# Two softmax heads handled as a pair: transposes, copy, reciprocal and buffers of the attention stage of a two-layer trunk

## What is computed

```python
def one_block(args):                       # MLA, dense and causal
    qb, t0 = args
    q_pos = t0 + jnp.arange(Q_BLOCK)
    logits = jnp.einsum('bqhd,bshd->bhqs', qb, k).astype(jnp.float32) * scale
    visible = key_pos[None, :] <= q_pos[:, None]
    logits = jnp.where(visible[None, None], logits, NEG_INF)
    p = jax.nn.softmax(logits, axis=-1).astype(v.dtype)
    return jnp.einsum('bhqs,bshd->bqhd', p, v)
```

## Time and profile before

| | us |
|---|---|
| median of three runs | 1304.08 (1303.95 to 1306.27) |
| profiled execution, its own time | 1305.61 |
| its span, first to last instruction | 1303.9 |
| TensorE busy | 1255.1 (96% of the span) |
| VectorE busy | 773.8 (59%) |
| ScalarE busy | 540.4 (41%) |
| mean granted TensorE clock | 0.995 of full |

### The profile page before, as it was taken

The page is one execution under the profiler, slowest core; times in us unless marked ns, Lnnn a source line. Parts: engine busy times, 40 slices in busy tenths (PEclk is TensorE's granted clock), DMA queues, the critical chain, the costliest instruction groups (busy, mean ns, idle before and its releaser), DMA issues.

```text
span 1303.9 us, 19103 instructions
## 1 busy us (share of the span) xinstructions
PE 1255.1 (96%) x5916; PEld 983.1 (75%) x5916; DVE 773.8 (59%) x1240; ACT 540.4 (41%) x871; POOL 247.1 (19%) x157
## 2 busy tenths in 40 slices
PE   4999999899999999999999999988999999999997
PEld 3856777578888888888877568765888888888886
DVE  4579866734454454444766888575445445445458
ACT  4474435834413314224436643376442242231343
POOL 4022340011020020110531324200201201102016
PEclk9999999999999999999999999999999999999999
DMA  5312220023222222222232112200233223222223
GB/s 200 101 49 65 65 98 1 2 65 110 97 96 97 97 97 97 97 97 97 97 99 81 56 59 82 65 2 2 97 125 97 97 96 97 96 96 98 96 98 129
DMA packets 31023, 110.46 MB, mean 85 GB/s; under 512 B 3568, under 2 KB 3568, under 8 KB 30960
## 3 DMA queue, kind: packets, MB, share of 16 engines
q1 hardware_dynamic: 29088, 103.82, 24.0%
q0 software_dynamic: 576, 3.76, 0.8%
q10 hardware_dynamic: 1296, 2.12, 0.5%
HBM read 107.59 MB, written 2.10 MB: 84 GB/s over the span
## 4 chain that ended last, share of the span: by engine, by line
PE 89%; DVE 3%; ACT 3%; issue 3%; POOL 1%; DMA 1%; DVEq 0%; ACTq 0%; SPq 0%; POOLq 0%
PE bank L824 18%; PE bank L823 18%; PE bank L822 18%; PE bank L477 6%; PE bank L479 6%; PE bank L478 6%; PE bank L511 2%; PE bank L500 2%; PE bank L498 2%; PE bank L499 2%; PE bank L709 1%; PE bank L736 1%; PE bank L721 1%; PE bank L693 1%; POOL lnb L410 1%
## 5 line engine op out<-in xcount | busy, mean ns | idle before, releaser
L877 ACT ACTIVATE wh<-raw 128x1024 fp32r<-128x1024 f32 x194 | 204.8, 1056 | 397.3 <-PE bank L824 239.0
L1165 DVE TENSOR_TENSOR wl<-raw,wh 128x1024 fp32r<-128x1024 f32 x158 | 247.2, 1565 | 102.6 <-ACT wh L877 95.1
L822 PE MATMUL bank<-hh,wl 128*128 128x512 f32 x512 | 200.0, 391 | 0.0
L822 PE MATMUL bank<-xmh,wl 128*128 128x512 f32 x512 | 199.3, 389 | 0.0
L824 PE MATMUL bank<-hl,wh 128*128 128x512 f32 x512 | 199.2, 389 | 0.0
L824 PE MATMUL bank<-xml,wh 128*128 128x512 f32 x512 | 199.2, 389 | 0.0
L823 PE MATMUL bank<-xmh,wh 128*128 128x512 f32 x512 | 199.2, 389 | 0.0
L823 PE MATMUL bank<-hh,wh 128*128 128x512 f32 x512 | 199.2, 389 | 0.0
L445 POOL TENSOR_TENSOR x<-x,rsb 128x512 f32<-128x512 f32 x64 | 84.6, 1322 | 580.3 <-DVE rsb L1555 580.3
L477 PE MATMUL bank<-xgh,wl 128*128 128x512 f32 x368 | 152.7, 415 | 23.5 <-DVE xgl L1174 18.3
L1544 DVE TENSOR_TENSOR sqb<-tf 128x512 f32<-128x512 f32 x64 | 44.3, 693 | 181.3 <-ACT hh L1136 181.3
(11 more groups left out here) (190 smaller groups left out, 1747.6 us busy)
## 6 DMA issues: line engine op xcount, KB each, us to landing
raw<-in_stream SPq DMA_DIRECT2D x194, 512.0 KB, 3.3
x<-in_x ACTq DMA_DIRECT2D x8, 256.0 KB, 12.5
out_y<-x SPq DMA_DIRECT2D x8, 256.0 KB, 4.3
par<-in_params POOLq DMA_DIRECT2D x2, 916.0 KB, 4.9
con<-in_consts POOLq DMA_DIRECT2D x1, 944.5 KB, 9.2
par<-in_params POOLq DMA_DIRECT2D x1, 896.0 KB, 11.4
par<-in_params ACTq DMA_DIRECT2D x1, 20.0 KB, 1.8
```

Source lines behind the costliest of these rows:

```text
L822: pe.matmul(B.t[s][:], wl[:, s, n_block(k)], src_h[:, k], start=(k == 0), stop=False)
L877: act.activation(wh[:, s], raw[:, s], ACT.Copy).then_inc(hi_ready.sem, 1)
L1165: vec.tensor_tensor(wl[:, s], raw[:, s], wh[:, s], ALU.subtract).then_inc(lo_ready.sem, 1)
```

## The change

Slots are handled two at a time. T becomes `turn_pair`: both heads' blocks go into banks 4 and 5, which are one tensor `banks45`, and there is one use (`pt0` to `pt15`) instead of one for each slot. C becomes one copy of both banks. N becomes one reciprocal of 128x2 and the two products, behind a wait for both sums. Planes of probabilities go from four to six, of transposes they stay four. On TensorE the sums of squares go ahead of `gla_out` and W. The first output unit waits for the last copy by name.

```diff
-LEAD, LAG, PLANES = 3, 2, 4
+LEAD, LAG, PLANES = 3, 2, 6
-    + [(f"pt{j}", 4 + j % 2) for j in range(N_ATT)]
+    + [(f"pt{p}", 5) for p in range(N_ATT // 2)]
-        self.t = [ctx.enter_context(nc.psum_tensor(f"bank{b}", [P, T], F32)) for b in range(8)]
+        self.t = [ctx.enter_context(nc.psum_tensor(f"bank{b}", [P, T], F32)) for b in range(4)]
+        self.both = ctx.enter_context(nc.psum_tensor("banks45", [P, 2, T], F32))
...
-        place("mpad", [P, 2, T])
+        pb3, _ = place("pb3", [P, 2, T])
-        pt2, _ = place("pt2", [P, T], at=xh0 + 4 * MIXED[-1] * T)
-        pt3, _ = place("pt3", [P, T], at=xl0 + 4 * MIXED[-1] * T)
+        pt2, _ = place("pt2", [P, 2, KB * T], at=xh0 + 4 * MIXED[-1] * T)
...
-                def turn(j):
-                    name = f"pt{j}"
+                def turn_pair(j):
+                    name = f"pt{j // 2}"
                     pe.wait_ge(*B.vacant(l, name))
-                    pe.wait_ge(*pn_ready.at(l, j))
-                    for kb in range(part_of(j)[1] + 1):
-                        m = pe.transpose(B[name][:, kb * P:(kb + 1) * P],
-                                         probs(j)[:, kb * P:(kb + 1) * P], ident)
+                    if j == 0:
+                        pe.wait_ge(*B.freed(l, "inc00"))
+                    for hp in range(2):
+                        pe.wait_ge(*pn_ready.at(l, j + hp))
+                        for kb in range(part_of(j)[1] + 1):
+                            m = pe.transpose(B.both[:, hp, kb * P:(kb + 1) * P],
+                                             probs(j + hp)[:, kb * P:(kb + 1) * P], ident)
                     m.then_inc(*B.on_fill(name))
...
-                    pe.wait_ge(*B.freed(l, f"pt{j}"))
-                    pe.wait_ge(*B.freed(l, f"pt{j + 1}"))
+                    pe.wait_ge(*B.freed(l, f"pt{j // 2}"))
...
                         pe.wait_ge(*B.vacant(l, name))
+                        pe.wait_ge(*B.freed(l, f"pt{N_ATT // 2 - 1}"))
                     for n in range(n0, n1):
...
-                    if j < N_ATT:
-                        turn(j)
+                    if j % 2 == 1 and j < N_ATT:
+                        turn_pair(j - 1)
+                    if j in STAT_SLOT:
+                        h = STAT_SLOT[j]
+                        stat(l, f"gst{h}", ones[:], sq_of(f"gst{h}"))
+                    if j % PAIR == LAG + 3 and j > PAIR:
+                        b = j // PAIR - 1
+                        stat(l, f"aost{b}", blk, sq_of(f"aost{b}"))
                     if j in OUT_SLOT:
                         gla_out(OUT_SLOT[j])
                     if j >= LAG and (j - LAG) % 2 == 1:
                         weigh_pair(j - LAG - 1)
                     if j % 2 == 0 and N_MLA <= j + PAIR_LEAD < N_ATT:
                         logits_pair(j + PAIR_LEAD)
...
-                def turned(j):
+                def turned_pair(j):
                     n = (part_of(j)[1] + 1) * P
-                    act.wait_ge(*B.filled(l, f"pt{j}"))
-                    if j >= PLANES:
-                        act.wait_ge(*weighed.at(l, j - PLANES))
-                    act.activation(probs_t(j, n), B[f"pt{j}"][:, 0:n], ACT.Copy)\
-                        .then_inc(*B.on_read(f"pt{j}"))
+                    act.wait_ge(*B.filled(l, f"pt{j // 2}"))
+                    if j >= 4:
+                        act.wait_ge(*weighed.at(l, j - 3))
+                    act.activation(probs_t(j, n), B.both[:, :, 0:n], ACT.Copy)\
+                        .then_inc(*B.on_read(f"pt{j // 2}"))
...
-                    turned(j)
+                    if j % 2 == 1:
+                        turned_pair(j - 1)
...
-                        vec.wait_ge(*B.filled(l, f"pt{j - PLANES}"))
+                        vec.wait_ge(*B.filled(l, f"pt{(j - PLANES) // 2}"))
...
-                def normalise(j):
+                def normalise_pair(j):
                     n = (part_of(j)[1] + 1) * P
-                    vec.wait_ge(*p_ready.at(l, j))
-                    link(vec.reciprocal(rinv[:, j:j + 1], rsum[:, j:j + 1]))
-                    vec.tensor_scalar(probs(j, n), probs(j, n), rinv[:, j:j + 1], None, ALU.mult)\
-                        .then_inc(pn_ready.sem, 1)
+                    vec.wait_ge(*p_ready.at(l, j + 1))
+                    link(vec.reciprocal(rinv[:, j:j + 2], rsum[:, j:j + 2]))
+                    for i in (j, j + 1):
+                        vec.tensor_scalar(probs(i, n), probs(i, n), rinv[:, i:i + 1], None, ALU.mult)\
+                            .then_inc(pn_ready.sem, 1)
...
-                normalise(0)
+                normalise_pair(0)
                 for j in range(N_ATT):
-                    if j + 1 < N_ATT:
-                        normalise(j + 1)
+                    if j % 2 == 1 and j + 1 < N_ATT:
+                        normalise_pair(j + 1)
                     if j + LEAD < N_ATT:
                         mask_max(j + LEAD)
```

More of the change, by code:

```diff
@@ L163, in __init__ @@
             self.fills[b] += name not in NO_FILL
-        self.t = [ctx.enter_context(nc.psum_tensor(f"bank{b}", [P, T], F32)) for b in range(8)]
+        self.t = [ctx.enter_context(nc.psum_tensor(f"bank{b}", [P, T], F32)) for b in range(4)]
+        self.both = ctx.enter_context(nc.psum_tensor("banks45", [P, 2, T], F32))
+        self.t += [self.both[:, i] for i in range(2)]
+        self.t += [ctx.enter_context(nc.psum_tensor(f"bank{b}", [P, T], F32)) for b in (6, 7)]
         self.fill = [ctx.enter_context(nc.semaphore(f"bank{b}_filled")) for b in range(8)]
@@ L288, in probs @@
             i = j % PLANES
-            return pb[:, i, 0:n] if i < 2 else pb2[:, i - 2, 0:n]
+            return (pb, pb2, pb3)[i // 2][:, i % 2, 0:n]
         def probs_t(j, n=T):
-            return (ptb[:, 0, 0:n], ptb[:, 1, 0:n], pt2[:, 0:n], pt3[:, 0:n])[j % PLANES]
+            return (ptb, pt2)[j // 2 % 2][:, :, 0:n]
         def gain(c, lo=0, hi=P):
@@ L736, in weigh_pair @@
                             m = pe.matmul(B[name][hp * 64:(hp + 1) * 64, qb * P:(qb + 1) * P],
-                                          v[:, kb, h * DH:(h + 1) * DH], probs_t(j + hp)[:, kb * P:(kb + 1) * P],
+                                          v[:, kb, h * DH:(h + 1) * DH], probs_t(j)[:, hp, kb * P:(kb + 1) * P],
                                           start=(kb == 0), stop=(kb == qb))
@@ L795, in _ @@
                         logits_pair(j + PAIR_LEAD)
[L796 to L801, removed]
                     if j in FIRST_OUT:
```

## The result

The changed kernel takes 1315.47 us (median of six runs, 1313.56 to 1316.48); the kernel before, run beside it, 1305.08 us. The ratio is 1.0073, with a 95% interval of 1.0058 to 1.0088: about 9.5 us slower by the ratio (the two medians differ by 10.4 us). Forecast were 1313 us and slower, from a sum of +9.0 us.

What follows compares the result with a forecast made beforehand. TensorE, busy 96% of the span, bounds the kernel; N's wait would bind in attention. Terms -0.4 + 5.8 - 0.95 give +4.5 us a layer, +9.0 us for two, against 1304.1 us: 1313 us, range 1304.5 to 1318 us.

Steps and rivals of the forecast that it cites:

- case C: Attention stage: N's wait for both exps of its pair makes the kernel slower, 1313 us; chance 0.57.
- rival D: Attention stage: TensorE waiting in every pair loses its clock too, 1.5 to 3 us a layer over the forecast; chance 0.1.
- The wait of N: VectorE, DSA pairs: over 12 us a layer idle before the reciprocal; one loop turn 3.38 us at 512 columns.
- Where TensorE waits: Sign in the profile after: TensorE idle before the transposes; no such waits in the DSA half would mean wrong.
- From N of slot 17 to N of slot 31: Pairs 18 to 30 of the attention stage: 23.4 us where 17.6 us were, +5.8 us a layer.
- Before slot 17: Earlier slots: TensorE gains about 1.8 us by slot 7, then the loop uses it up; -0.4 us a layer.
- C: ScalarE's copy of both banks: two copies occupy 0.94 us, one 0.96 us; taken as 0.
- T: TensorE, DSA half: each transpose group saved is worth 0.15 us, 1.2 us a layer, only where TensorE is waited for.
- Sums of squares: Last sum starts before W of slots 26, 27; the factor ahead of the last C comes 0.8 to 1.0 us sooner.
- The term of the tail: From N of slot 31 to the output unit: 2.6 us becomes 1.65 us, -0.95 us a layer.
- The price of N: Attention stage, pairs 18 to 30: the loop through N's wait costs +5.8 us a layer.
- Rival E: New queue order costs more, as T waiting for the previous pair's C: 1 us at four widest pairs, 1321 us; chance 0.05.

Runs made afterwards that it cites:

- experiment 1: Changed kernel with N alone put back to one reciprocal and one product per slot: 1300.42 us, ratio 0.9956 to the kernel before.
- experiment 3: Changed kernel with N of a pair one slot later, a maximum again between: 1301.66 us, ratio 0.9971 to the kernel before.
- experiment 2: Kernel before with N alone paired, in the order of the change: 1322.73 us, ratio 1.0132.
- experiment 4: Changed kernel with the sums of squares back in their old place: 1321.2 us, ratio 1.0115 to the kernel before.
- experiment 6: Changed kernel with single N and late sums of squares, leaving paired T and C with six planes: 1309.57 us, ratio 1.0038 to before.
- experiment 5: Kernel before with only the sums of squares moved ahead of `gla_out`: 1304.41 us, ratio 0.9999.

## Why the prediction was right, and where it was not

The likeliest case C happened, with a part of rival D.

- *The wait of N.* Right, in kind and size: 18.5 and 16.8 us of idle time before the reciprocal in the two layers, where "over 12 us" was given. One turn of the loop is 3.36 and 1.92 us (3.38 and 1.94). At 512 columns its parts are 0.73 us from M to exp, 1.55 us for both exps and 1.08 us for N, where the sum had 0.76, 1.62 and 1.0. Experiments 1 and 3 take it away and 2 makes it alone.
- *Where TensorE waits.* Wrong. I had it idle in front of the transposes, and called their absence a sign of being wrong. It is idle there for 0.2 us in layer 0 and 0.7 us in layer 1, less than the 2.1 and 2.2 us before. It waits in front of L, 3.7 us for M and 2.4 us for Ln in layer 0 (4.9 and 2.8 in layer 1; before 1.0, all for Ln). M reads the bank that L needs and stands behind N's wait, so the lock-step reaches TensorE by way of M and L, not of N and T. The cost of a turn is the same.
- *From N of slot 17 to N of slot 31.* It ends at 239.3 us (238.84 + 0.48; forecast 239.1) and 263.9 us (262.5): 24.6 us against 23.4. Of the 1.2 us too few, 1.1 is one place: the reciprocals of slots 24 and 26 lie 5.15 us apart in layer 0, where T and L ran at 1.2 GHz, and 4.05 us in layer 1 (896.51 to 900.56) at full clock. In that turn of layer 0 C was not covered by other work, as I had taken it to be: it waited 2.41 us for the slow T, and E of slot 26, whose maximum was there at 254.69, came behind it at 256.44.
- *Before slot 17.* TensorE did get ahead, by 2.6 us at the logits of slot 11 (220.60 against 223.25), and all of it was gone by slot 16, as forecast.
- *C.* One copy of 1024 columns takes 1.02 us and its successor starts after 0.92 us: two single ones took 0.94. Taken at 0, right. By the Trainium skill (ScalarE: Activation LUTs, What ACT_TABLE_LOAD costs) I had estimated a saving of 93 ns a pair; these rows give 0.02 us.
- *T.* Eight transposes take 1.03 us to the next start (256.77 to 257.80) where two groups of four took 1.16: 0.13 us saved, 0.15 forecast. In the sum T and C stood at 0, as TensorE waits anyway, and in the lock-step that holds: experiments 2 and 4 differ by paired T and C and the planes alone, and are at 1.0132 and 1.0115 with intervals that overlap. Without the lock-step it fails: there I expected 0 to -2 us and measured +5 (experiment 6). The greater part of that goes with a lower clock of TensorE, which I had not counted there, and why it falls is open.
- *Sums of squares.* The term of the tail is right to 0.01 us: 265.51 - 263.87 = 1.64 us after 2.58 us. The whole is mis-sized: 5.5 us in the changed kernel (experiment 4), not 1.9, and nothing measurable in the kernel before (experiment 5). Taken in the order N (experiment 2), T and C (4), sums (the change), the parts are +17, -2 and -5.5 us where I had 10.8, 0 and -1.9. The errors in N and in the sums are of opposite sign, and that the total still came out is in part luck, in part because I had followed the queues with the early sums in place: there a turn of the loop and the tail were right one by one.
- *The price of N.* I had it as 5.8 us a layer less what the loop gives back. Against the best that the rest of the change can do it is 1.0073 - 0.9956 = 1.2%, 7.6 us a layer.
- *The clock.* Rival D had a chance of 0.1 and 1.5 to 3 us a layer. In the profile the clock did fall in each stage, and I had forecast it unchanged; the four of six runs with a mean clock under 0.995 are longer by 1 to 1.5 us a layer, less than D's price. The Trainium skill (TensorE: Matmul & The Clock Gate, HAM oscillation) tells of frequent short idle times that bring the clock down. The trace agrees in part: falls follow idle times of 1.45 and 2.45 us in layer 0, and none follows the same two in layer 1.
- *Rival E*, T waiting for C of the pair ahead, shows once in a layer: 0.8 us.

## What to carry to other kernels

Before two waits on one engine are merged into one, look at what stood between a producer and its consumer. Here one exp had one VectorE operation beside it in the old order and none in the new; the pair itself was harmless one slot later. And an edit that groups work on one engine moves everything behind the group: paired transposes and early sums of squares were worth +0.4% and 0 alone, and -0.4% together, a part of it along with TensorE's clock, so single edits in such a schedule should be tried in both surroundings.

## What was not expected of the hardware

In the experiment with single N, TensorE's clock falls in 228 to 240 us (0.76, 0.50 and 0.89 by stretches of 4 us) though the view shows it busy for 15.45 of 16 us in 230 to 246 us, more than the 13.92 us of the kernel before at full clock, with 96 matmuls in it where there were 99. Instructions last longer at the lower clock, so a full row of busy time was here a sign of a slower TensorE and not of more work; such a row is to be read with the clock beside it. Nor was a fall there the ruin of a version: experiments 1 and 3 have one and are faster than before all the same.
